# Recurrent inverse: VectorE writes identity minus a level's first product, ScalarE copies the two products that follow

## The reference, cut to what matters

```python
def step(state, inp):
    r_t, w_t, k_t, v_t, kk_t, a_t = inp
    sa = jnp.einsum('bhij,bhj->bhi', state, -kk_t)
    state = (state * w_t[:, :, None, :] + sa[..., None] * (kk_t * a_t)[:, :, None, :]
             + v_t[..., None] * k_t[:, :, None, :])
    return state, jnp.einsum('bhij,bhj->bhi', state, r_t)

_, y = lax.scan(step, jnp.zeros((b, h, n, n), jnp.float32), xs, reverse=reverse)
```

## Time and profile before

| | |
|---|---|
| median of 3 runs | 2548.95 us (2546.47 to 2549.86) |
| the profiled execution, its own time | 2548.45 us |
| its span on the core | 2546.7 us |
| TensorE, VectorE, ScalarE busy | 2484.2, 1439.2, 527.6 us |
| pair stage of layer 0 / layer 1 | 206 to 345 us / 841 to 981 us |

### The profile page before, as it was taken

The page is one execution under the profiler, slowest core; times in us unless marked ns, Lnnn a source line. Parts: engine busy times, 40 slices in busy tenths (PEclk is TensorE's granted clock), DMA queues, the critical chain, the costliest instruction groups (busy, mean ns, idle before and its releaser), DMA issues. The chain is left out here.

```text
span 2546.7 us, 38463 instructions
## 1 busy us (share of the span) xinstructions
PE 2484.2 (98%) x15968; PEld 1905.6 (75%) x15968; DVE 1439.2 (57%) x2688; ACT 527.6 (21%) x1249; POOL 316.1 (12%) x367
## 2 busy tenths in 40 slices
PE   8999999999999999999999999999999999999998
PEld 7887886854788788685477747888886666666997
DVE  1576655855157655573357735555334488854775
ACT  1342220100134222010014910000003243411000
POOL 2002102110100210221000000000000155410110
PEclk9999999999999999999999999999999999999999
DMA  7331125987433212598632022222222534334553
GB/s 269 116 116 63 57 81 170 303 292 256 147 116 117 68 52 84 179 306 289 239 125 67 2 66 71 96 83 75 91 87 69 165 101 135 121 102 146 167 173 107
DMA packets 253603, 341.80 MB, mean 134 GB/s; under 512 B 7252, under 2 KB 179412, under 8 KB 253304
## 3 DMA queue, kind: packets, MB, share of 16 engines
q1 hardware_dynamic: 241632, 311.71, 37.4%
q10 hardware_dynamic: 8920, 17.67, 2.1%
q0 software_dynamic: 2880, 9.96, 1.0%
HBM read 338.13 MB, written 1.19 MB: 133 GB/s over the span
## 5 line engine op out<-in xcount | busy, mean ns | idle before, releaser
L1058 PE MATMUL PS<-MEM 128*128 128x256 f32 (+1 forms) x2632 | 447.9, 332 | 2.6 <-ACT MEM L1515 1.2
L1058 PEld LDWEIGHTS PS<-MEM 128*128 128x128 f32 x2632 | 406.3, 190 | 43.8 <-issue 1.9
L416 PE MATMUL PS<-MEM 128*128 128x256 f32 x1632 | 356.0, 379 | 0.0
L1474 ACT ACTIVATE MEM<-PS 128x256 f32<-128x256 f32 (+4 forms) x405 | 162.0, 429 | 907.8 <-PE PS L416 221.1
L416 PEld LDWEIGHTS PS<-MEM 128*128 128x128 f32 x1632 | 308.6, 190 | 42.5 <-issue 1.3
L462 PE MATMUL PS<-MEM 128*128 128x512 f32 x608 | 265.4, 597 | 9.1 <-DMA MEM<-w_down 4.3
L2094 DVE SCALAR_TENSOR_TENSOR MEM<-MEM 128x512 f32<-128x512 f32 x280 | 214.4, 798 | 53.7 <-DMA MEM<-ada_w 48.0
L462 PEld LDWEIGHTS PS<-MEM 128*128 128x128 f32 x608 | 115.3, 191 | 155.3 <-issue 141.2
L3038 POOL TENSOR_TENSOR MEM<-MEM 128x1 f32<-128x1 f32 (+1 forms) x34 | 21.6, 637 | 1269.4 <-DVE MEM L2040 812.1
L696 PE MATMUL PS<-MEM 128*128 128x256 f32 x768 | 178.3, 384 | 0.0
L1371 PE MATMUL PS<-MEM 128*128 128x512 f32 (+1 forms) x512 | 171.5, 488 | 0.0
(11 more groups left out here) (384 smaller groups left out, 3259.8 us busy)
## 6 DMA issues: line engine op xcount, KB each, us to landing
MEM<-w_in SPq DMA_DIRECT2D x54, 1024.0 KB, 5.4
MEM<-ada_w SPq DMA_DIRECT2D x48, 1024.0 KB, 7.5
MEM<-w_up SPq DMA_DIRECT2D x32, 1024.0 KB, 5.4
MEM<-w_down SPq DMA_DIRECT2D x32, 1024.0 KB, 5.1
MEM<-ssm_w_in SPq DMA_DIRECT2D x24, 1024.0 KB, 5.4
MEM<-ffn_gate SPq DMA_DIRECT2D x22, 1024.0 KB, 5.3
MEM<-ffn_up SPq DMA_DIRECT2D x22, 1024.0 KB, 5.4
MEM<-ffn_down SPq DMA_DIRECT2D x20, 1024.0 KB, 5.1
```

Source lines behind the costliest of these rows:

```text
L416: ins = pe.matmul(bank[:, 0:T], W[:, k, c * P:(c + 1) * P], XT[:, k, :], start=k == 0, stop=k == KT - 1)
L1058: ins = pe.matmul(out, left[:, k, :], right[:, k, :], start=k == 0, stop=k == 3)
L1474: act.activation(out, view(b), func, **kw).then_inc(S("bank_read_by_act"), 1)
```

## The change

The level is written the other way round. VectorE reads `Z` and writes identity minus `Z` into `ZI` (`level_left`). The two products that follow are then the new inverse and its transpose themselves, and ScalarE copies them into `UC` and `XI`; at level 5 it copies both halves of `XI` and the even group's block of `AB`, and VectorE the odd group's (`last_diagonal`). TensorE's instructions and their order are the same; who reads each bank is not. `begin_lefts` no longer waits for the last `dx`.

```diff
--- before.py
+++ after.py
@@ -810,7 +810,7 @@
                 def four_blocks(gs, keys, by, left, right, halves=(0, HB)):
 
-                    banks = [take(key, by) for key in keys]
+                    banks = [take(key, who) for key, who in zip(keys, by)]
...
-                    four_blocks(gs, [("Z", l, g, m) for g in gs], "act", lambda g: UM[g % 2][:, m % 2, :, :], lambda g: UC[g % 2])
+                    four_blocks(gs, [("Z", l, g, m) for g in gs], ("dve", "dve"), lambda g: UM[g % 2][:, m % 2, :, :], lambda g: UC[g % 2])
...
-                    four_blocks(gs, [("dx", l, g, m) for g in gs], "dve", lambda g: XI[g % 2], lambda g: ZI[g % 2])
+                    four_blocks(gs, [("dx", l, g, m) for g in gs], ("act", "act" if m < LEVELS - 1 else "dve"), lambda g: XI[g % 2], lambda g: ZI[g % 2])
...
-                    four_blocks(gs, [("dxt", l, g, m) for g in gs], "dve", lambda g: ZI[g % 2], lambda g: XI[g % 2], (0, HB) if m < LEVELS - 1 else (0,))
+                    four_blocks(gs, [("dxt", l, g, m) for g in gs], ("act", "act"), lambda g: ZI[g % 2], lambda g: XI[g % 2], (0, HB) if m < LEVELS - 1 else (0,))
...
@@ -1669,6 +1669,30 @@
+                def finer(g):
+
+                    if m < LEVELS - 1:
+                        copy(("dx", l, g, m), flat(UC[g % 2][:, :, :]), lambda b: b[:, 0:256])
+                    elif g % 2 == 0:
+                        b = filled(act, "act", ("dx", l, g, m))
+                        bv = b[:, 0:256].rearrange("p (i n) -> p i n", i=4)
+                        act.activation(AB[g % 4][0:HB, :, 0:HB], bv[0:HB, :, :], ACT.Copy)
+                        act.activation(AB[g % 4][HB:P, :, HB:P], bv[HB:P, :, :], ACT.Copy).then_inc(S("bank_read_by_act"), 1)
+
+                def finer_turned(g):
+
+                    b = filled(act, "act", ("dxt", l, g, m))
+                    x = flat(XI[g % 2][:, :, :])
+                    if m == LEVELS - 1:
+                        peek(act, ("dx", l, g, m))
+                        o = HB * (g % 2)
+                        act.activation(x[o:o + HB, :], b[o:o + HB, 0:256], ACT.Copy).then_inc(S("bank_read_by_act"), 1)
+                    elif g % 2:
+                        act.activation(x[0:HB, :], b[HB:P, 0:256], ACT.Copy)
+                        act.activation(x[HB:P, :], b[0:HB, 0:256], ACT.Copy).then_inc(S("bank_read_by_act"), 1)
+                    else:
+                        act.activation(x, b[:, 0:256], ACT.Copy).then_inc(S("bank_read_by_act"), 1)
...
                     for m in range(1, LEVELS):
-                        for g in gs:
-                            copy(("Z", l, g, m), flat(ZI[g % 2][:, :, :]), lambda b: b[:, 0:256])
...
                         slot(("z", m))
+                        for step in (finer_turned, finer) if m == LEVELS - 1 else (finer, finer_turned):
+                            for g in gs:
+                                step(g)
                         slot(("x", m))
...
@@ -2373,41 +2398,22 @@
                         emptied(dve, ("sl", l, g, 1))
-                        if g > 1:
-                            emptied(dve, ("dx", l, g - 2, LEVELS - 1))
                         ins = begin_left(g)
...
-                def finer(g):
-
-                    b = filled(dve, "dve", ("dx", l, g, m))
+                def level_left(g):
+
+                    b = filled(dve, "dve", ("Z", l, g, m))
+                    read(dve.tensor_tensor(ZI[g % 2][:, :, :], eye, b[:, 0:256].rearrange("p (i n) -> p i n", i=4), ALU.subtract))
+
+                def last_diagonal(g):
+
+                    b = filled(dve, "dve", ("dx", l, g, LEVELS - 1))
                     bv = b[:, 0:256].rearrange("p (i n) -> p i n", i=4)
...
+                    dve.tensor_copy(AB[g % 4][0:HB, :, 0:HB], bv[0:HB, :, :])
+                    read(dve.tensor_copy(AB[g % 4][HB:P, :, HB:P], bv[HB:P, :, :]))
...
                     for m in range(1, LEVELS):
+                        for g in gs:
+                            level_left(g)
                         slot(("z", m))
-                        for step in (finer_turned, finer) if m == LEVELS - 1 else (finer, finer_turned):
-                            for g in gs:
-                                step(g)
+                        if m == LEVELS - 1:
+                            last_diagonal(gs[1])
                         if m in (1, 2):
                             masked("sk", AK, gs[m - 1])
```

More of the change, by code:

```diff
@@ L2381, in begin_lefts @@
                         dve.tensor_tensor(UC[g % 2][:, :, :], eye, UC[g % 2][:, :, :], ALU.subtract)
-                def finer(g):
-                    b = filled(dve, "dve", ("dx", l, g, m))
-                    bv = b[:, 0:256].rearrange("p (i n) -> p i n", i=4)
[L2387 to L2410, removed]
+                def level_left(g):
[3 more added lines that the diff above has]
+                    b = filled(dve, "dve", ("dx", l, g, LEVELS - 1))
+                    bv = b[:, 0:256].rearrange("p (i n) -> p i n", i=4)
+                    dve.tensor_copy(AB[g % 4][0:HB, :, 0:HB], bv[0:HB, :, :])
+                    read(dve.tensor_copy(AB[g % 4][HB:P, :, HB:P], bv[HB:P, :, :]))
                 pair = 0
```

## The result

The changed kernel takes 2553.93 us (median of 15 runs), the kernel before, timed beside it, 2548.87 (15 runs): a ratio of 1.0021 with a 95% interval of 1.0013 to 1.0029, or 3.3 to 7.4 us slower. One of the 15 runs of the kernel before took 2891.09 us; the ratio leaves it out. The forecast was 2553.0 us, or +4.5 us between profiled executions. The profiled execution of the changed kernel takes 2551.49 us, the lowest of its 15, with a span of 2549.7 us, 3.0 above that of before.

A forecast was written before the change was run, and what follows sets the result against it. TensorE, busy 2484.2 of 2546.7 us, was taken to bound the kernel, so only its waits count. Terms 2.6 + 2.7 - 0.8 = +4.5 us on the profiled 2548.45 gave 2553.0 us; range 2546.5 to 2560.

The forecast's parts named there:

- the doubtful number: Time from a level's first scores load to the start of `masked`: 1.16 us, in place of 1.59.
- The rival in which `masked` starts no sooner: Scores, not VectorE's subtractions, held `masked`, so it stays at 1.59 us; 2561 us in all; chance 0.12.
- The rival in which it starts well before 1.16: `masked` starts earlier, so the place in VectorE's queue costs next to nothing; 2546.5 to 2551 us, no change; chance 0.20.
- 1.16 + 1.29 + 0.75 - 0.08 + 0.18: New step from scores to next `level_x`: `masked` start, `masked`, `level_left`, their overlap, release of `level_x`; 3.30 us.
- kind B: Four steps, level 1 into 2 of pairs 2 and 3: from 2.63 to 3.30 us each, +2.7 us.
- Kind A: Nine steps of pairs 0 and 1 with `right_side` or `keys_turned` next, no gate work: 3.01 to 3.30 us, +2.6 us.
- kind C: Five steps where TensorE has enough work of its own: 3.31 us, change 0, margin 0.01 to 0.08.
- the fifth step: The kind C step of pair 0, layer 0, level 1 into 2, at 3.38 us before; change 0 forecast.
- `keys_flipped`: In pair 0, once a layer, it waits for `masked` alone: 2.91 to 2.50 us, -0.8 us in all.
- the second rival: ScalarE's five copies take 475 ns each and become late; `right_side` waits, kind C pays 1.5 us; 2554.5 us; chance 0.10.
- Faster: TensorE falls back to its own path everywhere: 2543.5 us, 0.21% below the median; chance 0.08.

The follow-up runs named there:

- e3: Changed kernel with level 2 of pairs 2 and 3 in the form of the kernel before; 2554.80 us in one execution.
- e8: Changed kernel with the two loops of scores exchanged, the first bank's products issued before the second's; 2554.22 us, ratio 1.0019 to the kernel before.
- e12: Changed kernel with the loops of scores exchanged and both products of the second bank made twice; 2573.06 us in one execution.
- e1: Changed kernel with `level_left` between the halves of `masked` at the four kind B steps alone; 2553.52 us in one execution.
- e4: Changed kernel with each half of `masked` in four instructions of 2x64 columns instead of one of 2x256; 2562.14 us in one execution.
- e2: Changed kernel with `level_left` ahead of both halves of `masked` at all Kind A and kind B steps and four of kind C; 2563.78 us, one execution.
- e7: Changed kernel with each ScalarE `dx` copy in two instructions and the even group's `dxt` copy in four; 2558.84 us in one execution.
- e6: As e5, but pair 1 alternates: levels 1 and 3 in the new form, 2, 4 and 5 old; 2546.93 us, ratio 0.9993 to the kernel before.
- e11: As e6, with `level_left` behind both halves of `masked` in pair 0; 2545.22 us, ratio 0.9985 to the kernel before.
- e5: Changed kernel with even group in old form; `level_left` between `masked` halves at Kind A and kind B steps; 2548.16 us, ratio 0.9996 to kernel before.
- e10: As e5, with the loops of scores exchanged and `level_left` behind both halves of `masked` at Kind A; 2548.01 us, ratio 0.9996 to the kernel before.

## Why the prediction was right

- **The start of `masked`, 1.16 us.** It was the doubtful number, and the earlier trace rows gave it: every step of kinds A and B shows 1.16 or 1.17. The rival in which `masked` starts no sooner (1.59, 2561 us) falls in every row; e3 brings the late start back (1.61 in the row shown) by putting the subtractions back. The rival in which it starts well before 1.16 falls too, and so does what spoke for it, that the first bank is full before the second: in e8 and e12 the two are filled side by side.
- **The queue.** 1.16 + 1.29 + 0.75 - 0.08 + 0.18 was put at 3.30; measured 3.29, with 1.17, 1.29, an overlap of 0.09, 0.74 and 0.18. e1 takes out 0.57 by moving half of `masked`, e4 puts in 0.39 by lengthening it, e2 shows that the other order only makes `masked` late. The new reader itself costs 0.09: in e2's kind B, where it waits for `Z` alone, the step is 2.72 where ScalarE's copies had 2.63.
- **The terms.** Kind A +2.6 (forecast +2.6), kind B +2.6 (+2.7), kind C 0 but for the fifth step's -0.07, `keys_flipped` -0.8 (-0.8). Sum +4.4 against +4.5; the timing has +3.3 to +7.4. The forecast of 2553.0 lies 0.9 below the median because it was made against a profiled execution 0.5 below the median of the runs then shown, and the rest is within what the runs of one kernel differ by.
- **ScalarE.** Five copies lie at 0.66 for the two of `dx`, 0.39, 0.38 and 0.38 us, as the row of the same operation in the earlier trace rows had it; no wait of `right_side` names them, and e7 puts the margin at 0.26 us where 0.2 was read. The 475 ns of the rival belong to another form: the sigmoid's row has a second operand from SBUF (`PS,MEM`), the copies have none. The Trainium skill (ScalarE: Activation LUTs, Rules for kernel authors) budgets about 0.3 us for an ACTIVATE whose bias is a [128,1] operand, and 0.83 ns for each element. For 256 columns that is an estimate of 0.51 us, which the sigmoid's 475 ns come near; it is no price for the copies, which took 382.
- **What the prediction overlooked.** It had `level_z` hidden from ScalarE by `scores`. In the last pair's level 4, which has no scores ahead of it, `level_z` waits for the two `dx` copies, and in e7, where they take 0.79 in place of 0.66, it starts 1.84 after `level_x` in place of 1.72. A wait of `level_z` for a ScalarE copy was named as a sign of the second rival; here it only replaces a longer wait for VectorE (1.81 before). That this wait got 0.1 us shorter and not longer was luck, since the prediction hadn't looked at it.
- **Faster** had 0.08 for a TensorE that falls back to its own work everywhere. The order denied it in the changed kernel; with the forms alternated, e6 and e11 reach it in pair 1 alone (2.72 where 2.66 was worked out).

Where expectations of mine failed, it was by three things. In e5 I let `level_left` start 0.08 before the half of `masked` ahead of it ends; it starts where that half ends, at 1.85 to 1.86, and the steps are 0.07 to 0.08 longer. `Z` is full only just then, which may be why; no run shows it. In e8, e10 and e12 I took it that the bank that is issued first is full first. In e4 and e7 I added up rows of single short instructions, which overlap when they follow one another.

## What to carry to other kernels

When a read of a product is moved to another in-order engine, price it by what stands ahead of it there at that moment, and not by its length or by how busy the engine is: here VectorE lost 47 us of work and TensorE waited longer. The sum of the rows in the queue, from the event that starts it to the release of the reader, came out to 0.01 us in the changed kernel (3.30 for 3.29), to 0.05 in e3 (3.73 for 3.74 and 3.68) and to 0.08 in e5. If each of two forms makes another engine late, alternate them, so that the engine that one form has freed meets the level of the other. The step at which both are late must then lie under other work: in e6 and e11 that is pair 1's step from level 2 into 3, which gate work holds at 4.65 us anyway.

## What the runs showed of the hardware

- Scores of two banks whose operands lie in the two halves of TensorE's rows run side by side, one matmul each 0.215 us in each half, whichever bank is issued first (starts in e8 and e12). So doubling one bank's products costs 0.87 us, not the 0.57 of two products more at the pace of the whole.
- Small instructions in a row overlap: four ScalarE copies of 128 columns take 0.79 us, where a lone one of that size takes 0.28, and eight pieces of `masked` 1.68 where two whole halves take 1.29. The sums of single rows would be 1.1 and 2.3.
- TensorE pauses with nothing to release it (behind `level_x` of pair 1's level 4, layer 0: 0.88 us before, 0.24 in the changed kernel, 1.00 in e11). What causes it stays open.
